# Four PSUM banks for the first expert product, four gathered rows ahead instead of ten, and the second set of normed rows copied out of SBUF

## The reference

```python
def chunk(hc):                                   # 128 tokens
    q = (hc @ wq).reshape(T, PEER_HEADS, 2, PEER_KEY_DIM)
    s1 = jnp.einsum('thd,hnd->thn', q[:, :, 0], sub_keys[:, 0])
    s2 = jnp.einsum('thd,hnd->thn', q[:, :, 1], sub_keys[:, 1])
    v1, i1 = lax.top_k(s1, PEER_TOPK)
    v2, i2 = lax.top_k(s2, PEER_TOPK)
    cand = (v1[..., :, None] + v2[..., None, :]).reshape(T, PEER_HEADS, PEER_TOPK * PEER_TOPK)
    sc, ci = lax.top_k(cand, PEER_TOPK)
    e = ...                                      # expert numbers, 8 heads x 16
    g = jax.nn.softmax(sc, axis=-1)
    act = jax.nn.gelu(jnp.einsum('td,thkd->thk', hc, exp_u[e]), approximate=False)
    w = g * act
    return jnp.einsum('thk,thkd->td', w, exp_v[e])
```

## Time and profile before

| | |
|---|---|
| median of 3 runs | 820.61 us (819.38 to 820.77) |
| the profiled execution's own time | 820.81 us |
| its span, from the first to the last instruction | 819.0 us |
| busy: TensorE 787.0 us (96%), VectorE 544.3 (66%), ScalarE 213.8 (26%), GpSimd 246.6 (30%) | |
| DMA | 294.31 MB, mean 359 GB/s |
| chain that ended last | PE 71%, DMA 21%, DVE 5% |

### The profile page before, as it was taken

The page is one execution under the profiler, slowest core; times in us unless marked ns, Lnnn a source line. Parts: engine busy times, 40 slices in busy tenths (PEclk is TensorE's granted clock), DMA queues, the critical chain, the costliest instruction groups (busy, mean ns, idle before and its releaser), DMA issues.

```text
span 819.0 us, 14745 instructions
## 1 busy us (share of the span) xinstructions
PE 787.0 (96%) x5726; PEld 754.2 (92%) x5726; DVE 544.3 (66%) x1165; ACT 213.8 (26%) x604; POOL 246.6 (30%) x224
## 2 busy tenths in 40 slices
PE   6999999899998999979999999999999999999996
PEld 4988779889998999979999998899999999999995
DVE  4958879878999795658898996564434343443423
ACT  4464476551211121324554451100000000000004
POOL 2000000000005447325445654253434433443400
PEclk9999999999999999989999999999999999999998
DMA  8998973468978999999999999999999999999971
GB/s 332 406 378 328 388 308 155 194 238 322 393 314 267 397 392 383 350 351 388 409 409 408 409 408 408 406 407 409 409 409 409 406 409 408 409 408 409 409 279 52
DMA packets 77216, 294.31 MB, mean 359 GB/s; under 512 B 8799, under 2 KB 11103, under 8 KB 75868
## 3 DMA queue, kind: packets, MB, share of 16 engines
q1 hardware_dynamic: 48614, 191.52, 59.7%
q0 software_dynamic: 28000, 101.23, 31.8%
q10 hardware_dynamic: 534, 0.62, 0.2%
HBM read 291.25 MB, written 1.56 MB: 358 GB/s over the span
## 4 chain that ended last, share of the span: by engine, by line
PE 71%; DMA 21%; DVE 5%; ACT 1%; issue 1%; another core or an unknown queue 1%; SPq 0%; ACTq 0%; DVEq 0%
PE banks L1256 28%; PE banks L1286 23%; DMA raw<-in_v_b 13%; DMA raw<-in_u_t 5%; PE banks L1001 3%; PE banks L1269 2%; PE banks L919 2%; PE banks L954 2%; PE banks L997 2%; DMA raw<-in_w_mod 2%; PE banks L1070 1%; PE banks L924 1%; DVE sc_w L1396 1%; PE banks L970 1%; PE banks L1159 1%
## 5 line engine op out<-in xcount | busy, mean ns | idle before, releaser
L1256 PE MATMUL banks<-hT,raw 128*128 128x160 f32 x2048 | 290.4, 303 | 10.2 <-DMA raw<-in_u_t 6.6
L1256 PEld LDWEIGHTS banks<-hT,raw 128*128 128x128 f32 x2048 | 282.9, 192 | 13.2 <-DMA raw<-in_u_t 9.5
L1286 PE MATMUL banks<-act,raw 128*128 128x160 f32 x2048 | 285.5, 300 | 1.2 <-DMA raw<-in_v_b 0.2
L1286 PEld LDWEIGHTS banks<-act,raw 128*128 128x128 f32 x2048 | 279.2, 190 | 6.5 <-DMA raw<-in_v_b 5.8
L1764 DVE SCALAR_TENSOR_TENSOR row_sums<-rows,weight,row_sums 128x1024 f32<-128x1024 f32 x94 | 120.8, 1285 | 142.1 <-DMA rows<-in_v_b,idx 140.7
L574 POOL DMA_INDIRECT rows<-in_v_b,idx x96 | 119.9, 1249 | 170.5 <-PE banks L1286 111.8
L574 POOL DMA_INDIRECT rows<-in_u_rows,idx x96 | 118.8, 1237 | 153.1 <-DVE dots L1741 95.0
L1741 DVE CUSTOM_DVE_ANT_0 rows<-rows,h_rows 128x1024 f32<-128x1024 f32 x96 | 114.7, 1221 | 7.3 <-DMA rows<-in_u_rows,idx 6.5
L851 ACT ACTIVATE turned<-banks,ccol 128x256 f32<-128x256 f32 x8 | 3.8, 472 | 283.9 <-PE banks L1286 283.9
L555 POOL DMA_DIRECT2D h_lines<-h_stage x1 | 0.5, 519 | 204.5 <-ACT h_stage L822 204.5
L782 ACT ACTIVATE act<-banks 128x160 f32<-128x160 f32 (+19 forms) x118 | 31.3, 267 | 111.4 <-PE banks L1256 94.6
(11 more groups left out here) (245 smaller groups left out, 788.7 us busy)
## 6 DMA issues: line engine op xcount, KB each, us to landing
raw<-in_u_t SPq DMA_DIRECT2D x128, 512.0 KB, 10.7
raw<-in_v_b SPq DMA_DIRECT2D x128, 512.0 KB
wq<-in_wq SPq DMA_DIRECT2D x2, 4096.0 KB, 18.2
sh_w<-in_w_mod SPq DMA_DIRECT2D x8, 512.0 KB, 13.0
sc_w<-in_w_mod SPq DMA_DIRECT2D x8, 512.0 KB, 13.8
win<-in_w_in SPq DMA_DIRECT2D x8, 512.0 KB, 14.2
win<-in_w_in SPq DMA_DIRECT2D x1, 4096.0 KB, 20.9
sc_w<-in_w_mod SPq DMA_DIRECT2D x2, 2048.0 KB, 23.8
```

The costliest lines, as they stand in the source:

```text
L1256: last = nc.tensor.matmul(dst, raw[spot_of[n]][:, c * P:(c + 1) * P], hT[:, c, 0:MANY], start=(c == 0), stop=(c == DC - 1))
L1286: return nc.tensor.matmul(chunk_place(c)[:, 0:MANY], raw[spot_of[BLOCKS + j]][:, c * P:(c + 1) * P], act[:, j, :], start=(j == 0 and c < 4 ...
```

## The change

The first product uses four banks (4, 5, 0, 1 in turn) in blocks 8 to 119, two before and after. `h2_rows[1]` is filled by four copies of 32 rows out of `h2_stage`, which ScalarE issues in its steps n = 50 and n = 52, two each; the store to DRAM and SP's load are gone. The expert numbers go out at step 16 instead of 17 and come in at 17 instead of 19. Of the second product's row tiles four instead of ten are gathered without a wait for blocks, then one per 1.32 blocks instead of 1.36.

```diff
-H2_LATER = (64,)
-EXPERTS_OUT = 17
-EXPERTS_IN = 19
+LATE_ROWS = (50, 52)
+EXPERTS_OUT = 16
+EXPERTS_IN = 17
...
-AHEAD = 10
-PACE = 1.36
+FOUR_BANKS = (8, 120)
+AHEAD = 4
+PACE = 1.32
...
+        def u_bank(n):
+
+            return (4, 5, 0, 1)[n % 4] if FOUR_BANKS[0] <= n < FOUR_BANKS[1] else 4 + n % 2
...
                 sp.dma_start(raw[spot_of[n]][:, :], u_t[n] if n < BLOCKS else v_b[n - BLOCKS]
                              ).then_inc(raw_full[spot_of[n]], 16)
-                if n in H2_LATER:
-                    kind = 1 + H2_LATER.index(n)
-                    count = KINDS[kind]
-                    sp.wait_ge(h2_saved, 16)
-                    sp.wait_ge(block_used, ROWS_AT)
-                    sp.dma_start(h2_rows[kind][:, :],
-                                 bass.AP(tensor=h2_lines, offset=KIND_AT[kind] * D,
-                                         ap=[[0, P // count], [D, count], [1, D]])).then_inc(h2_late, 16)
...
-            pool.wait_ge(xn_ready, TT + 3)
-            pool.dma_start(h2_lines.ap(), h2_stage[0:FEW, :]).then_inc(h2_saved, 16)
...
-                    last = nc.scalar.activation(gelu_out[:, n % 2, 0:before], bank[4 + n % 2][:, 0:before], ACT.Gelu)
+                    last = nc.scalar.activation(gelu_out[:, n % 2, 0:before], bank[u_bank(n)][:, 0:before], ACT.Gelu)
...
+                if n in LATE_ROWS:
+                    count = KINDS[1]
+                    for q in range(LATE_ROWS.index(n) * 2, LATE_ROWS.index(n) * 2 + 2):
+                        sc.dma_start(h2_rows[1][q * count:(q + 1) * count, :], h2_stage[KIND_AT[1]:KIND_AT[2], :]
+                                     ).then_inc(h2_late, 16)
...
             def u_block(n):
                 pe.wait_ge(raw_full[spot_of[n]], 16 * fills[n])
-                if n >= 2:
-                    pe.wait_ge(act_out, n - 1)
+                ahead = [m for m in range(n) if u_bank(m) == u_bank(n)]
+                if ahead:
+                    pe.wait_ge(act_out, ahead[-1] + 1)
+                elif n >= FOUR_BANKS[0]:
+                    pe.wait_ge(xn_ready, TT + 3)
...
-                dst = bank[4 + n % 2][:, 0:MANY]
+                dst = bank[u_bank(n)][:, 0:MANY]
...
-                    ve.wait_ge(h2_late, 16 + 16 * len(H2_LATER))
+                    ve.wait_ge(h2_late, 16 + 16 * (P // KINDS[1]))
```

More of the change, by code:

```diff
@@ L262, in hybrid_peer_layer @@
         scratch = nc.dram_tensor("bias_table", [MAPS, TABLE], F32, kind="Internal")
-        h2_lines = nc.dram_tensor("h2_lines", [FEW, D], F32, kind="Internal")
         expert_lines = nc.dram_tensor("expert_lines", [FEW, HK], U32, kind="Internal")
@@ L310, in hybrid_peer_layer @@
             sem, ("second_ready", "onehot_ready", "gates_ready", "gates_used", "gates_out"))
-        lines_moved, h2_saved = map(sem, ("lines_moved", "h2_saved"))
+        lines_moved = sem("lines_moved")
         gathered = [sem(f"gathered{n}") for n in range(SLOTS)]
@@ L779, in gelu @@
                         sc.wait_ge(late_act, n - GATE_AT - 2)
-                    last = nc.scalar.activation(gelu_out[:, n % 2, 0:before], bank[4 + n % 2][:, 0:before], ACT.Gelu)
+                    last = nc.scalar.activation(gelu_out[:, n % 2, 0:before], bank[u_bank(n)][:, 0:before], ACT.Gelu)
                 if before < MANY:
-                    last = nc.scalar.activation(act[:, n, before:MANY], bank[4 + n % 2][:, before:MANY], ACT.Gelu)
+                    last = nc.scalar.activation(act[:, n, before:MANY], bank[u_bank(n)][:, before:MANY], ACT.Gelu)
                 last.then_inc(act_out, 1)
```

## The result

The median went from 820.0 us (818.08 to 820.77, 4 runs on the chip of this comparison) to 809.76 us (808.46 to 810.35, 4 runs): ratio 0.987, 95% interval 0.9854 to 0.9885, so 1.3% faster. The forecast was 805.8, with a range of 798 to 812.5. The range held; the forecast was 4 us too low. The profiled execution is the fastest of the four: 808.46 us, with a span of 806.7.

A forecast was written before the change was run, and what follows sets the result against it. DMA, closely followed by TensorE, was taken as the bound: block 248 at 772.2 us, plus 8.7, 1.2 and an end of 22.05, gave a span of 804.2; plus 1.8 less 0.2, 805.8 us, range 798 to 812.5.

The forecast's parts named there:

- a: TensorE's loss around block 26: 2.79 us idle for a late Gelu plus 1.8 us of low clock, together 4.6 us.
- b: TensorE's loss at block 65: 5.50 us waiting for a weight block plus 3.4 us of low clock, together 8.9 us.
- c: TensorE's loss in blocks 120 to 127, each waiting for its block: 21.4 us instead of 17.4, 4.1 us.
- DMA's bytes are the only bound: Rival: the first product's gain turns into waits for blocks, block 128 starts at 520.25 as before, 825 us; chance 0.07.
- the six gathers: Gathers leaving the stretch of blocks 120 to 127 with four rows ahead instead of ten: 7.7 us of DMA.
- DMA gains 7.1 us of lead: Blocks 120 to 127 need only 10.3 us of DMA in 17.4; the lead pays 7.1 of 10.6 us later.
- d: Loss over 115 blocks of the second product, 256.7 us instead of 249.6: 7.1 us, half of it to go.
- the forecast's own ledger: DMA's account from block 57 to block 248: 346 units of 512 KB, 444.6 us, putting block 248 at 772.2 us.
- spread: Some DMA engines 3 units ahead of the slowest near the end; if from the odd read, 3.5 us comes back (0 to 3.9).
- the shortage at block 57: DMA must do 1 unit more in 4.6 us less by block 57: 2 us short, bounds 0 to 5.9.
- the row of the first set: Profile window of the first normed rows' copies, 215 to 225 us, at 376 GB/s: at most 0.8 us lost.
- a last row over 3 us late (then the clock falls too): Sign against the forecast, ahead of the sums over rows, where a wait of 0 to 1.6 us was expected.

The follow-up runs named there:

- run 2: The changed kernel with the second set of normed rows stored to DRAM and read back by SP after block 64, as before: 818.01 us, ratio 0.9983.
- run 4: The kernel before, with the one read of the second set of rows split into four reads of 32 rows from DRAM: 814.86 us, ratio 0.995.
- run 3: The changed kernel with two banks instead of four all through the first product: 810.36 us, ratio 0.9903.
- run 12: The kernel before with only the four banks of blocks 8 to 119 added: 819.8 us, ratio 0.9999.
- run 1: The changed kernel with ten rows gathered ahead and one per 1.36 blocks again: 812.08 us, ratio 0.9916.
- run 5: The kernel before with only the new pace, four rows ahead and one per 1.32 blocks: 817.95 us, ratio 0.9985.
- run 6: The changed kernel gathering only half of each row (512 of 1024 columns) in the second product: 798.24 us, ratio 0.9737.
- run 8: The changed kernel with the second rows' copies in steps 18 and 20 instead of 50 and 52, one place for weight blocks given up: 810.09 us, ratio 0.9875.
- run 7: The changed kernel with the expert numbers out at step 17 and in at 19 again: 813.46 us, ratio 0.9925.
- run 11: The changed kernel with pace 1.335 instead of 1.32, so the last row is gathered one block later: 814.93 us, ratio 0.9951.
- runs 9 and 10: The changed kernel with the sums one block later: 9 also has the second rows' copies in steps 18 and 20, 807.34 us; 10 does not, 809.33 us.

## Why the prediction was right, and where it was 4 us off

**Losses a, b and c going: right.** Block 128 was due at 333.5 - 4.6 + 186.8 - 8.9 - 4.1 = 502.7 us by the prediction's figures, and came at 503.2. That the old read made the 270 GB/s, and these the wait at block 65, is shown from both sides: put back in, it brings both (run 2); split up, it loses the wait and 3.1 of the 5.4 us (run 4). The rival "DMA's bytes are the only bound" fell with that. How the gain divides is another matter. The 4.6 us of the four banks are worth 0.6 to 2.7 with the rest in place (run 3), and nothing alone (run 12): TensorE's lead goes into later waits for DMA. And c was put down to the six gathers; with ten ahead it is gone too once the read is (run 1), and with the read split but ten ahead it stays (run 4: 510.9 - 489.6 = 21.3 us), while four ahead with the old read leaves 18.6 and 19.0 us (runs 5 and 2). Neither edit is its single cause: each takes a part of how late DMA was.

**The step that failed: "DMA gains 7.1 us of lead ... about 3.5 us of d stay, half of it goes".** d grew, from 7.1 to 10.4 us (271.2 against run 6's 260.8). In 485.8 to 503.2 us DMA did move what was promised: 17.4 x 408 = 7.1 MB, 13.5 units, for blocks that need 8. But SP was 8 blocks ahead at block 120 and 8 at block 128, since the places are no more, and POOL issued no new gather in that window (the last before it at 484.87 us, the next at 504.34). So the 5.5 units over were gathers already issued: the lead only emptied the queue of gathers and could not be stored. In run 5, also with four ahead, DMA wasn't even full in these blocks (340 GB/s at a share of 0.93), and nothing used what it had to spare. The second product then needed 120 x 1.758 = 211 units, 271.1 us, and took 271.2: none of it was paid from before. Nine blocks later, at 522.9 us, TensorE met DMA's pace. In the forecast's own ledger this is the credit of 3.5 us for the "spread": from 774.4 us on 7 blocks, 3 rows and the final gain were due, 11 units, and the windows moved (361 x 10 + 79 x 5.6) / 524 = 7.7. So some 3 units more had been moved than had landed, as before. The credit never came, so it wasn't the odd read that made it; whether it is some engines ahead of the slowest, as the prediction had it, no run shows.

**The ledger.** Its sum was right for partly wrong reasons: 346 units and 444.6 us forecast, 346.9 and 445.1 measured. Two gathers too many were counted in: of the 192 gathers 191 were issued at block 243 before and at block 248 after, and one unit less had been moved. That is 3 units, 3.9 us too much. In the other direction the shortage at block 57 was 4.7 us instead of 2: up to its start 108.8 MB had been moved before and 107.0 after, where 0.5 more were due for the rows and 0.4 fewer for the store, so 1.9 MB were missing; the copies' 1.9 us are a part of it. With the credit of 3.5 and block 57's 0.2: 772.2 + 3.5 + 2.7 - 3.9 + 0.2 = 774.7, measured 774.4; the 0.3 left are the rate and rounding. So the forecast of block 248 came within 2.2 us because errors of 2.7 to 3.9 us cancelled in part.

**The rows from SBUF.** Bounds 0 to 5.4 us gained, I took 5.4 by the row of the first set (376 GB/s; the same window after had 351). It is 5.4 - 1.9 = 3.5 net (run 8). That the copies cost more than the 0.8 us of that row may lie in the 32 partitions, in four copies instead of two or in what runs beside them; no run varies one of these alone. The Trainium skill, "SBUF — State Buffer", section "Door 1", was the rule against it; by its 218 GB/s the copies were an estimated 1.1 us slower than full rate. The runs agree in sign and show more, 1.9 us of DMA's time over the two pairs (325 GB/s with them, 377 without). They cost no wait of TensorE there; it shows 2.3 us later at block 248 (run 8).

**The numbers earlier.** "0 us, if not some DMA work drawn forward": it was drawn forward (the first gather from 252.5 to 246.2 us, where I had 248.4), and since DMA sets block 248, that is 2.6 us (run 7), and 3.7 in the median with the low clock at the end.

**The last row.** Wait 0.85 us, for 1.2 forecast and 1.6 at most. The start at which the criterion ends gives (774.4 to 779.6) 5.2 us, the wait and what follows take 1.4 back, and 2.3 to 3.8 remain (run 1). The sign "a last row over 3 us late (then the clock falls too)" set the point too high: it fell after 0.89 (run 8), 0.96 (run 7), 1.03 (run 5) and 1.24 us (run 2), and during the 3.37 of run 11, and not after 0.73 (run 3) and 0.85 (the change). Its cost was not in the sum.

**From the span to the median.** Block 248 +2.2, its end +0.3 (32.3 for 31.95): span 806.7 for 804.2. The execution is 1.76 us longer than its span, as forecast; but it is the fastest of four, 1.3 under their median, where I had taken it 0.2 above, after before's.

**Open.** Why a Gelu follows an idle time of 3.5 to 5.8 us instead of 1.87 around the first gathers (the releaser is "remote" or a product long done). It is in all 14 profiles; with two banks it stops TensorE, with four it doesn't. No run here separates it from the gathers, or from the loads of the expert numbers just before them. And what else spreads executions of one kernel over 4 us (runs 9 and 10) stays unsettled, having one profile of each.

## What to carry to other kernels

Where two bounds lie within 3% of each other, an edit's worth depends on the rest: banks, pace and read (split) give 0, 1 (within the noise) and 4 us alone, and cost 0.6 to 2.7, 2.3 to 3.8 and 8.3 to 9.3 when the old form is put back into the whole. Before crediting a transfer engine with a lead, ask where it would be stored: with all places of the ring full and the gathers paced, spare DMA time is not kept. And with DMA full, count a copy by the time in which it makes the rate fall, not by its bytes, and put it where the rate is low anyway (run 8: 2.3 us at block 248, which its profiled execution lost again at the end).

## What the runs showed of the hardware

- A read of 512 KB whose pattern has its 4 copies outermost lowered the rate to 270 GB/s for 16 us; as four reads of 32 rows it was 315 GB/s for 10 us. With copies out of 32 partitions of SBUF, 512 KB, it was 325 GB/s for 15 us, and 377 in the same window without them.
- A wait of TensorE of about 0.9 us, ahead of a stretch of narrow products (128 x 64), was followed by 6.8 us at the 1.2 GHz level in four profiled executions (waits of 0.89 to 1.24 us), 3.4 us lost; after 0.73 and 0.85 us it wasn't. Ahead of products of 128 x 160, around the first gathers, idle times of 0.90, 1.35, 2.18 and 2.26 us (runs 9, 3, 5 and 4) had no such loss; the 2.79 us before the change had.
- Around the first gathers ScalarE stood idle for 3.5 to 5.8 us instead of 1.87, in all 14 profiles. It seems to move with the gathers: the longest idle time ended 5.7 to 11.0 us after the first of them was issued (252.5 and 263.3 us before, 246.2 and 253.3 after).
